# Hybrid decoder trunk on one core: inputs stored feature-major, weights as one stream, values computed token-major ahead of the heads, scores in half-array pairs, heads unrolled in a new order

## The chip, the cores and the metric

One core of a Trainium2 chip. The metric is the device time of one execution in microseconds (us), median of several runs; lower is better. PE is TensorE, ACT ScalarE, DVE VectorE, POOL GpSimd, SP SyncE (it issues nearly all DMAs).

## The reference

Two layers, 512 tokens, 1024 features, float32. Layer 0 mixes by causal differential attention with 8 heads, layer 1 by pooled causal means over 2, 4, 8 and 16 tokens. Each layer goes on with a convolutional gated MLP (2816 wide) and a gated embedding; a final RMS norm ends it. The attention is the part that the change rewrites:

```python
qkv = xn @ w_qkv                                   # xn = rmsnorm(x, g), 512 x 1024
lam = exp(sum(lam_q1*lam_k1)) - exp(sum(lam_q2*lam_k2)) + lambda_init
s = einsum('bhcqd,bhckd->bhcqk', q_blk, k) * ATTN_SCALE   # 8 heads, components c = 0, 1, head_dim 64
a = softmax(where(causal, s, -inf))
w = a[:, :, 0] - lam * a[:, :, 1]
o = einsum('bhqk,bhkv->bhqv', w, v)                # v of a head is 128 wide
o = rmsnorm(o, sub_g) * (1 - lambda_init)
h = x + o.reshape(B, S, 1024) @ w_o
```

## The kernel before, in words

**Products.** Float32 products are made exact enough by splitting each operand into a high part (rounded to the matmul's 32-bit format, `_hi`) and the rest (`_lo`), and adding three matmuls: hi x hi, hi x lo, lo x hi (`exact`, lines 1182 to 1184). One call takes a 128x128 block of weights and 512 moving columns and accumulates in one of 8 PSUM banks.

**Weight units.** Weights come in units of up to 8 blocks (512 KB). SP loads a unit into `w_raw`; ACT writes `w_hi` (`split_hi`), then DVE writes `w_lo` (`split_lo`), and a counter `lo_done` lets PE use it. ACT and DVE do this at fixed places of their own instruction order, one or two units ahead of PE. Attention uses three slots (q, k, v of a head), everything later four.

**Order.** Each engine has its own written-out order, and semaphores tie them. The start (`start_rest` and the lines ahead of `head`): x arrives token-major, PE transposes it (L1219, 32 transposes), ACT and DVE make `x_hi` and `x_lo` scaled by the gain; parameters and p are also transposed on PE (L1319, L1327). The token norm is not applied to x: its inverse goes into the softmax scale and into k and v (multiplied by `inv`, a 128x512 tile that PE spreads from a diagonal, L1301/L1302).

Then 8 heads, each on PE: q projection (24 matmuls), k projection (24), transposes of the last head's v (4, L1270) and of its softmax weights (10, L1278), the spread of the norm of the head before that (L1301), v projection (24), the last head's product weights x v (`head_product`, 12), this head's scores, and within them the sums of squares for the last head's output norm (L1296). Heads 2 to 7 are a hardware loop.

**Scores** (lines 1251 and 1253). `q_hi` holds for each component c its 64 rows and a copy in the other 64; `k_hilo` holds k's high part in the one half and its low part in the other. So one matmul with 128 rows gives q_hi x (k_hi + k_lo), and a second adds q_lo x k_hi: two matmuls for each query tile (width 128, 256, 384, 512) and component, plus masks as bf16 matmuls with an identity (L1256, L1259) behind them.

**After the heads.** The output projection `wo` has 8 units. Its first three accumulate over the finished heads while head 7's softmax, weights, product and norm are still under way; `wo_part(m, heads)` is one such piece. Everything after it (embedding, MLP, pooling, second layer) is some 900 us of matmuls that the change leaves as they are, except for a counter's offsets.

## Time and profile before

| what | value |
| --- | --- |
| median of 3 runs | 1131.6 us (1131.04 to 1131.61) |
| the profiled execution | 1132.1 us, its span 1130.4 us |
| PE busy | 1111.5 us (98%), 5201 matmuls |
| DVE, ACT busy | 753.7 us (67%), 559.8 us (50%) |
| granted PE clock, mean | 0.995 of full speed |
| DMA | 103.57 MB, 92 GB/s on average |

The span is what the profile covers; 1.7 us lie around it. Busy PE time counts pipelined matmuls with a modelled end, so that the distance between two starts says what a matmul really takes. The heads lie between 13.8 and 208.5 us, the output projection behind them.

### The profile page before, as it was taken

How to read it: one execution, taken by the hardware profiler on the slowest of the kernel's cores; microseconds unless marked ns; L12 is line 12 of the kernel's file. 1: busy time of each engine (PE TensorE's matmuls, PEld its weight loads, DVE VectorE, ACT ScalarE, POOL GpSimd, SP SyncE). 2: the span in 40 equal slices, each digit the busy share in tenths (PEclk: the TensorE clock that was granted, in tenths of full speed). 3: DMA queues.
4: the chain of work that ended last, by engine and by line, in shares of the span. 5: the costliest groups of instructions: out<-in, count | busy, mean ns of one | idle time of the engine just before them, and what ended most of it. 6: DMA issues, size and time to landing. Idle time of an engine off the chain costs nothing.

```text
span 1130.4 us, 14839 instructions
## 1 busy us (share of the span) xinstructions
PE 1111.5 (98%) x5201; PEld 924.4 (82%) x5201; DVE 753.7 (67%) x1080; ACT 559.8 (50%) x832; POOL 9.0 (1%) x57
## 2 busy tenths in 40 slices
PE   7999999999999999999999999999999999999996
PEld 6888888888888888888888888888888888888885
DVE  5878788765776347752676787777537774476773
ACT  7777776746554224431444577544314442244564
POOL 0000000002000000000000000000000000000000
PEclk9999999999999999999999999999999999999998
DMA  7232113132333423333323432133323333232411
GB/s 218 70 88 61 56 56 93 57 104 83 93 93 100 120 79 93 93 113 92 93 75 98 126 93 76 57 97 108 112 75 93 98 107 112 75 88 84 126 38 75
DMA packets 192544, 103.57 MB, mean 92 GB/s; under 512 B 3651, under 2 KB 190452, under 8 KB 192500
## 3 DMA queue, kind: packets, MB, share of 16 engines
q1 hardware_dynamic: 192484, 102.99, 30.9%
q8 instruction: 26, 0.43, 0.2%
q14 instruction: 18, 0.15, 0.0%
q10 hardware_dynamic: 16, 0.00, 0.0%
HBM read 100.89 MB, written 2.10 MB: 91 GB/s over the span
## 4 chain that ended last, share of the span: by engine, by line
PE 96%; ACT 1%; DMA 1%; DVE 0%; issue 0%; SPq 0%; ACTq 0%
PE bank L1182 30%; PE bank L1184 30%; PE bank L1183 30%; PE bank L1251 1%; PE bank L1253 1%; PE bank L1296 1%; DMA x_tok<-in_x 1%; PE bank L1278 1%; PE bank L1475 0%; PE bank L1270 0%; PE bank L1472 0%; PE bank L1207 0%; PE bank L1301 0%; PE bank L1302 0%; PE bank L1256 0%
## 5 line engine op out<-in xcount | busy, mean ns | idle before, releaser
L1182 PE MATMUL bank<-x_hi,w_hi 128*128 128x512 f32 x1024 | 400.9, 391 | 1.5 <-DVE h L798 1.5
L1184 PE MATMUL bank<-x_hi,w_lo 128*128 128x512 f32 x1024 | 399.3, 390 | 0.0
L1183 PE MATMUL bank<-x_lo,w_hi 128*128 128x512 f32 x1024 | 399.0, 390 | 0.0
L1182 PEld LDWEIGHTS bank<-x_hi,w_hi 128*128 128x128 f32 x1024 | 192.7, 188 | 41.3 <-issue 1.7
L1184 PEld LDWEIGHTS bank<-x_hi,w_lo 128*128 128x128 f32 x1024 | 192.5, 188 | 40.3
L1183 PEld LDWEIGHTS bank<-x_lo,w_hi 128*128 128x128 f32 x1024 | 192.7, 188 | 39.6
L423 ACT ACTIVATE w_hi<-w_raw 128x1024 fp32r<-128x1024 f32 (+1 forms) x166 | 169.5, 1027 | 102.9 <-PE bank L1184 102.9
L781 DVE TENSOR_TENSOR w_lo<-w_raw,w_hi 128x1024 fp32r<-128x1024 f32 (+1 forms) x166 | 198.0, 1194 | 33.7 <-ACT w_hi L423 33.5
L1182 PE MATMUL bank<-g_hi,w_hi 128*128 128x512 f32 x352 | 136.9, 389 | 0.0
L1183 PE MATMUL bank<-g_lo,w_hi 128*128 128x512 f32 x352 | 136.9, 389 | 0.0
L1184 PE MATMUL bank<-g_hi,w_lo 128*128 128x512 f32 x352 | 136.9, 389 | 0.0
L677 ACT ACTIVATE c<-u,params 128x512 f32<-128x512 f32 x88 | 71.9, 817 | 107.6 <-DVE u L1104 107.6
L1104 DVE TENSOR_TENSOR u<-bank,inv 128x512 f32<-128x512 f32 x88 | 60.7, 689 | 93.3 <-PE bank L1184 93.2
L1002 DVE TENSOR_TENSOR h<-bank,h 128x512 f32<-128x512 f32 x56 | 38.5, 688 | 97.9 <-PE bank L1184 97.9
L684 ACT ACTIVATE g_hi<-g 128x512 f32 (+1 forms) x44 | 27.8, 633 | 118.4 <-DVE g L1120 118.4
L1182 PEld LDWEIGHTS bank<-g_hi,w_hi 128*128 128x128 f32 x352 | 66.1, 188 | 13.7
L1183 PEld LDWEIGHTS bank<-g_lo,w_hi 128*128 128x128 f32 x352 | 66.1, 188 | 13.7
L1184 PEld LDWEIGHTS bank<-g_hi,w_lo 128*128 128x128 f32 x352 | 66.1, 188 | 13.7
L1114 DVE SCALAR_TENSOR_TENSOR c<-u,params,c 128x512 f32<-128x512 f32 x88 | 66.2, 752 | 9.7 <-DVE c L1109 0.9
L1109 DVE SCALAR_TENSOR_TENSOR c<-u,params,c 128x512 f32<-128x512 f32 x88 | 66.0, 750 | 2.3 <-ACT c L677 0.9
L682 ACT ACTIVATE s<-c 128x512 f32<-128x512 f32 x44 | 27.8, 633 | 74.6 <-DVE c L1114 74.6
L1122 DVE TENSOR_TENSOR g_lo<-g,g_hi 128x512 f32 (+1 forms) x44 | 30.5, 693 | 37.7 <-ACT g_hi L684 37.7
(196 smaller groups left out, 1116.1 us busy)
## 6 DMA issues: line engine op xcount, KB each, us to landing
w_raw<-in_w_up SPq DMA_DIRECT2D x88, 512.0 KB, 3.8
w_raw<-in_w_down SPq DMA_DIRECT2D x32, 512.0 KB, 3.5
w_raw<-in_w_qkv SPq DMA_DIRECT2D x24, 512.0 KB, 4.4
w_raw<-in_w_ple_gate SPq DMA_DIRECT2D x16, 512.0 KB, 3.5
w_raw<-in_w_down SPq DMA_DIRECT2D x16, 384.0 KB, 3.1
w_raw<-in_w_attn_out SPq DMA_DIRECT2D x8, 512.0 KB, 3.7
x_tok<-in_x SPq DMA_DIRECT2D x4, 512.0 KB, 5.3
w_raw<-in_w_ple_proj SPq DMA_DIRECT2D x4, 512.0 KB, 4.0
```

Of the source, the lines that this page charges most:

```text
L423: act.activation(w_hi[s][:, 0:w], w_raw[s][:, 0:w], ACT.Copy).then_inc(hi_done, 1)
L677: act.activation(c32[:, c, :], u32[:, c, PAD:PAD + SEQ], ACT.Identity, scale=tap(layer, 2, j + c * FT), bias=conv_bias(layer, j + c * FT)) ...
L682: act.activation(s32[:, :], c32[:, 0, :], ACT.Silu).then_inc(silu_done, 1)
L781: dve.tensor_tensor(w_lo[s][:, 0:w], w_raw[s][:, 0:w], w_hi[s][:, 0:w].bitcast(F32), ALU.subtract).then_inc(lo_done, 1)
L1002: dve.tensor_tensor(h[:, m, :], src, h[:, m, :], ALU.add).then_inc(evac_done, 1)
L1104: dve.tensor_tensor(u32[:, c, PAD:], bank[2 * v + c][:, :], inv[:, :], ALU.mult).then_inc(evac_done, 1)
L1109: dve.scalar_tensor_tensor(out=c32[:, c, :], in0=u32[:, c, PAD - 1:PAD - 1 + SEQ], scalar=tap(layer, 1, j + c * FT), in1=c32[:, c, :], op0 ...
L1114: dve.scalar_tensor_tensor(out=c32[:, c, :], in0=u32[:, c, PAD - 2:PAD - 2 + SEQ], scalar=tap(layer, 0, j + c * FT), in1=c32[:, c, :], op0 ...
L1122: dve.tensor_tensor(g_lo[:, 2 * a + v, :], g32[:, :], g_hi[:, 2 * a + v, :].bitcast(F32), ALU.subtract).then_inc(glo_done, 1)
L1182: pe.matmul(dst, w1, m1, start=start and i == 0, stop=False)
L1183: pe.matmul(dst, w1, m0, start=False, stop=False)
L1184: last = pe.matmul(dst, w0, m1, start=False, stop=stop and i == len(parts) - 1)
```

## The change

**Layout.** The host hands over x and p feature-major, the parameters as one table of columns, and all weights as one array of 166 units of 128 x 1024, in the order of use. PE's transposes of x, p and the parameters are gone; x goes by DMA straight into `h`. The sum of squares of x, before an accumulating ACT pass over `x_tok`, is now made like the other norms: squares on ACT, adds on DVE, then `token_sums` on PE.

**v first.** The first 8 units are v's weights. Tokens are the stationary side, so v comes out token-major for all heads (2 groups of 4 heads, 8 steps k of 12 matmuls each: 192 matmuls, as many as before) and needs no transposes. The inverse norm is a scale per partition (`value_high`, `value_low`). Then each head projects k, then q; a ring of four slots serves all units.

**Scores.** q and k are stored once. Three half-array matmuls (64 rows) for each query tile and component: q_hi x k_hi, q_hi x k_lo, q_lo x k_hi, component 0 on rows 0 to 63 and component 1 on rows 64 to 127, into different banks, issued in turn. The masks go first.

**Softmax.** The weights are kept unnormalized: ratio = lam * sum0 / sum1, w = ratio*a1 - a0, one DVE pass in place of two; a term with sum0 squared goes into the output norm's epsilon (`output_variance`), and the sign into `sub_g_scaled`.

**Order.** The heads are unrolled, the softmax weights are transposed in the middle of the q projection, and the last head's pieces of `wo` are put in another order.

```diff
@@ score banks and matmuls
-                return bank[2 + qt][:, c * w:(c + 1) * w]
+                return bank[2 + c][:, qt * P:qt * P + w]
...
-                        pe.matmul(dst, q_hi[:, c, keys], k_hilo[:, c, 0:w], start=not (shared and c), stop=False,
-                                  skip_group_check=shared)
-                        pe.matmul(dst, q_lo[:, c, keys], k_hilo[:, c, 0:w], start=False, stop=False, skip_group_check=shared)
...
+                    for q, k, stop in ((q_hi, k_hi, False), (q_hi, k_lo, False), (q_lo, k_hi, True)):
+                        for c in range(2):
+                            last = pe.matmul(scores_at(qt, c), q[half[c], keys], k[half[c], 0:w], start=False, stop=stop,
+                                             skip_group_check=True)
@@ ACT between the value groups
+            split_hi(4)
+            rms_of(NORM_MIX0)
+            act.wait_ge(icol_done, 1)
+            for t in range(TT):
+                value_high(t)
+            split_hi(5)
+            inverse(NORM_MIX0)
+            act.wait_ge(p_in, 16)
+            for j in range(DEPTH * PLE_KT):
+                act.activation(pT_hi[:, j, :], p_raw[:, j, :], ACT.Copy).then_inc(pT_hi_done, 1)
+                if j == 0:
+                    split_hi(6)
@@ PE, the values
+            for k in range(1, KT):
+                values(0, k)
+            pe.wait_ge(acc_done, KT)
+            token_sums(bank[7], acc).then_inc(ss_done, 1)
+            for k in range(KT):
+                values(1, k)
+                if k == 3:
+                    pe.wait_ge(diag_done, 1)
+                    pe.wait_ge(vlo_done, 1)
+                    spread(bank[0]).then_inc(spread_done, 1)
@@ PE, a head
+            for hd in range(N_HEADS):
+                n = FIRST_KQ + 2 * hd
...
+                project(bank[1], n, range(KT))
...
+                    project(bank[0], n + 1, range(0, KT // 2))
                     head_transposes(hd - 1)
+                    project(bank[0], n + 1, range(KT // 2, KT))
+                if hd >= 2:
+                    output_spread(hd - 2)
+                if hd >= 1:
+                    pe.wait_ge(k32_done, hd + 1)
+                    head_product(hd - 1, bank[1])
+                scores(hd)
+                if hd >= 1:
+                    output_sums(hd - 1, bank[0])
@@ DVE, a head
+            for hd in range(N_HEADS):
+                split_lo(FIRST_KQ + 2 * hd + 2)
+                k_rows(hd)
+                if hd >= 2:
+                    output_inverse(hd - 2)
+                k_low(hd)
+                if hd >= 1:
+                    transposed_low(hd - 1)
+                split_lo(FIRST_KQ + 2 * hd + 3)
+                q_low(hd)
+                if hd >= 2:
+                    output_norm(hd - 2)
+                    output_low(hd - 2)
+                softmax_first(hd)
+                if hd >= 1:
+                    output_variance(hd - 1, bank[0])
+                softmax_second(hd)
@@ ACT and PE, the last head
+            output_rms(last - 1)
+            transposed_high(last)
+            split_hi(PHASES["wo"][0] + 2)
+            output_high(last - 1)
+            output_square(last, bank[2])
+            output_copy(last, bank[2])
+            split_hi(PHASES["wo"][0] + 3)
...
+            head_transposes(last)
+            output_spread(last - 1)
+            wo_part(2, range(0, last - 1), start=True)
+            head_product(last, bank[2])
+            wo_part(3, range(0, 2), start=True)
+            output_sums(last, bank[4])
+            wo_part(3, range(2, last - 1))
```

How the order stands on the engines at three places. **First**, ACT where the norm of x is turned into a tile, before: the tile `inv` comes behind q's high part, and no unit of weights that PE wants next stands behind it.

```order
L429 ACTIVATE w_hi<-w_raw 128x1024 [waits raw_in2]
L480 ACTIVATE q_hi<-bank 64x512 [waits unit_done]
L480 ACTIVATE q_hi<-bank 64x512
L483 ACTIVATE q_hi<-q_hi 64x512 [waits qhi_done] x2
L437 ACTIVATE inv<-bank 128x512 [waits spread_done]
L488 ACTIVATE k_hilo<-k 64x512 [waits k32_done]
```

Now, ACT at the same tile (`w_hi2` there is unit 6, which PE uses at step k = 4 of the second group of values):

```order
L351 ACTIVATE w_hi1<-w_raw1 128x1024 [waits unit_done,raw_in1]
L359 ACTIVATE inv<-bank0 128x512 [waits spread_done]
L406 ACTIVATE pT_hi<-p_raw 128x512 [waits p_in]
L351 ACTIVATE w_hi2<-w_raw2 128x1024 [waits unit_done,raw_in2]
L406 ACTIVATE pT_hi<-p_raw 128x512 x3
```

The split of unit 6 stands behind the tile, and the tile waits for the spread, which PE issues after step k = 3, right ahead of step k = 4.

**Second**, PE at the scores of heads 2 to 7, before (k and q are the moving and the stationary side):

```order
L1182 MATMUL bank6<-wT_hi,v_hi 128x128 [waits wtlo_done]
...
L1251 MATMUL bank2<-k_hilo,q_hi 128x128 [waits wtlo_done]
L1253 MATMUL bank2<-k_hilo,q_lo 128x128
...
L1259 MATMUL bank2<-mask16,ident16 128x256
...
L1251 MATMUL bank6<-k_hilo,q_hi 128x512 [waits onorm_done,o32_done]
```

and now:

```order
L1080 MATMUL bank1<-wT_hi,v_hi 128x128 [waits wtlo_done]
...
L1187 MATMUL bank2<-mask16,ident16 128x2x128 [waits onorm_done,klo_done,qlo_done]
L1187 MATMUL bank3<-mask16,ident16 128x2x128
L1191 MATMUL bank4<-mask16,ident16 128x128
...
L1197 MATMUL bank2<-k_hi,q_hi 128x128
L1197 MATMUL bank3<-k_hi,q_hi 128x128
```

The first score matmul now waits for `onorm_done` (the normed output of two heads before, for its bank 6) and `qlo_done`; before, `onorm_done` was waited for four query tiles later.

**Third**, PE in the last head, before:

```order
L1182 MATMUL bank6<-wT_hi,v_hi 128x512 [waits wtlo_done,vlo_done]
...
L1182 MATMUL bank2<-oT_hi,w_hi1 128x512 [waits lo_done,wtlo_done]
...
L1301 MATMUL bank7<-diag,ones_r 128x512 [waits odiag_done,onorm_done]
L1302 MATMUL bank7<-diag,ones_r 128x512
L1182 MATMUL bank3<-oT_hi,w_hi2 128x512 [waits lo_done]
```

PE now, and ACT beside it:

```order
L1117 MATMUL bank6<-diag,ones_r 128x512 [waits odiag_done]
L1118 MATMUL bank6<-diag,ones_r 128x512
L1080 MATMUL bank7<-oT_hi,w_hi2 128x512 [waits lo_done]
...
L1080 MATMUL bank2<-wT_hi,v_hi 128x512 [waits wtlo_done]
...
L1080 MATMUL bank3<-oT_hi,w_hi3 128x512 [waits lo_done]
```

```order
L428 ACTIVATE wT_hi<-bank2 128x512 [waits w_T]
L428 ACTIVATE wT_hi<-bank3 128x384 [waits w_T]
L428 ACTIVATE wT_hi<-bank4 128x384 [waits w_T]
L351 ACTIVATE w_hi2<-w_raw2 128x1024 [waits unit_done,raw_in2]
L434 ACTIVATE oT_hi<-acc 128x512 [waits onorm_done]
L438 ACTIVATE sq<-bank2 128x512 [waits pv_done]
L445 ACTIVATE acc<-bank2,small 128x512 [waits olo_done]
L351 ACTIVATE w_hi3<-w_raw3 128x1024 [waits unit_done,raw_in3]
```

The third piece of `wo` (bank 7, `w_hi2`) moved ahead of the head's product and its weights are split behind the transposed softmax weights; the fourth (bank 3, `w_hi3`) moved to right behind the product, and its weights are split behind the square that waits for that product.

## Rows read from the trace of the kernel before

**Rows 1.** The page, part 1: busy us (share of the span), instructions.

```profile
PE 1111.5 (98%) x5201; PEld 924.4 (82%) x5201; DVE 753.7 (67%) x1080; ACT 559.8 (50%) x832; POOL 9.0 (1%) x57
```

**Rows 2.** Waits of PE: line and releaser: us, times, longest.

```profile
PE bank L1182 <- DVE h L798: 1.5, 1, 1.5
PE bank L1182 <- DVE wT_lo L939: 0.5, 1, 0.5
```

**Rows 3.** Timeline (start us, us, operation), start; window with clock, its seventh entry.

```profile
4.26 1.06 ACT L446 ACTIVATE square_scratch<-x_tok 128x1024 f32<-128x1024 f32 x1 [1.54 <-DMA x_tok<-in_x]
13.77 0.77 PE L1182 MATMUL bank<-x_hi,w_hi 128*128 128x512 f32 x1 [1.50 <-DVE h L798]
16.47 0.51 PE L1182 MATMUL bank<-x_hi,w_hi 128*128 128x512 f32 x1
...
14.00:16.00 2.00, 2.00 (x5) 1.56 (x6) 1.97 (x4) 2.00 (x5) 0.00 (x0) 0.50 0.15 37
```

**Rows 4.** Timeline of PE through one head.

```profile
123.77 0.39 PE L1182 MATMUL bank<-x_hi,w_hi 128*128 128x512 f32 x1
129.24 0.39 PE L1182 MATMUL bank<-wT_hi,v_hi 128*128 128x512 f32 x1
131.10 0.27 PE L1251 MATMUL bank<-k_hilo,q_hi 128*128 128x128 f32 x1
132.26 0.95 PE L1296 MATMUL bank<-ones,sq 128*128 128x1 f32 x8
133.08 0.42 PE L1251 MATMUL bank<-k_hilo,q_hi 128*128 128x384 f32 x1
135.22 0.48 PE L1182 MATMUL bank<-x_hi,w_hi 128*128 128x512 f32 x1
```

**Rows 5.** Timeline, PE: transposes and spread ahead of Rows 4.

```profile
121.77 0.60 PE L1270 MATMUL bank<-ident,vT 128*128 128x128 f32 x4
122.21 1.25 PE L1278 MATMUL bank<-ident,probs 128*128 128x128 f32 x10
123.22 0.48 PE L1301 MATMUL bank<-diag,ones_r 128*128 128x512 f32 x1
```

**Rows 6.** Timeline, end of the start: spread, parameters, lambda.

```profile
26.39 0.39 PE L1302 MATMUL bank<-diag,ones_r 128*128 128x512 f32 x1
26.82 0.60 ACT L437 ACTIVATE inv<-bank 128x512 f32<-128x512 f32 x1 [1.74 <-PE bank L1302]
28.83 0.29 PEld L1332 LDWEIGHTS bank<-lam_rows,ones 64*128 64x128 f32 x2 [0.17 <-issue]
29.14 0.50 PE L1182 MATMUL bank<-x_hi,w_hi 128*128 128x512 f32 x1
```

**Rows 7.** Timeline of the same head, ACT.

```profile
134.07 1.28 ACT L519 ACT_TABLE_LOAD   x1
135.36 0.46 ACT L519 ACTIVATE probs<-bank,small 128x128 f32<-128x128 f32 x1
137.33 0.68 ACT L519 ACTIVATE probs<-bank,small 128x384 f32<-128x384 f32 x1
140.14 1.08 ACT L429 ACTIVATE w_hi<-w_raw 128x1024 fp32r<-128x1024 f32 x1
```

**Rows 8.** Timeline of the same head, DVE.

```profile
132.53 1.02 DVE L889 TENSOR_REDUCE small<-bank 128x2 f32<-128x256 f32 x2 [0.80 <-PE bank L1259]
135.44 1.29 DVE L893 TENSOR_REDUCE small<-bank 128x1 f32<-128x512 f32 x2 [0.16 <-PE bank L1256]
143.99 1.23 DVE L787 TENSOR_TENSOR w_lo<-w_raw,w_hi 128x1024 fp32r<-128x1024 f32 x1
145.14 0.17 DVE L944 RECIPROCAL small<-small 128x4 f32<-128x4 f32 x1
147.00 0.69 DVE L875 TENSOR_TENSOR k<-bank,inv 128x512 f32<-128x512 f32 x1
150.44 1.61 DVE L939 TENSOR_TENSOR wT_lo<-bank,wT_hi 128x512 fp32r<-128x512 f32 x3
```

More of the change, by code:

```diff
@@ L279, in hybrid_trunk @@
         sums = small[:, 32:40]
-        rsums = small[:, 40:48]
+        sums_of = [sums.rearrange("p (t c) -> p t c", c=2)[:, :, c] for c in range(2)]
+        rsum = small[:, 40:44]
+        ratio = small[:, 44:48]
         rms_col = small[:, 48:52]
@@ L477, in q_high @@
-            def q_high(hd):
-                act.wait_ge(unit_done, 3 * hd + 1)
-                for c in range(2):
-                    act.activation(q_hi[own[c], c, :], bank[0][own[c], :], ACT.Copy).then_inc(qhi_done, 1)
-                for c in range(2):
-                    act.wait_ge(qhi_done, 2 * hd + c + 1)
-                    act.activation(q_hi[other[c], c, :], q_hi[own[c], c, :].bitcast(F32), ACT.Copy).then_inc(qtwin_done, 1)
+                act.activation(inv[:, :], bank[7 if norm else 0][:, :], ACT.Copy, scale=float(D_MODEL)).then_inc(inv_done, 1)
@@ new lines, in token_sums, with spread @@
+            def token_sums(dst, squares):
+                for t in range(TT):
+                    last = pe.matmul(dst[:, t:t + 1], squares[:, t * P:(t + 1) * P], ones[:, 0:1], start=True, stop=True)
+                return last
+            def spread(dst):
+                pe.matmul(dst[:, :], ones_r[:, :], diag[:, 0, :], start=True, stop=False)
+                return pe.matmul(dst[:, :], ones_r[:, :], diag[:, 1, :], start=False, stop=True)
+            TOK = [slice(t * P, (t + 1) * P) for t in range(TT)]
@@ L1409, in norm_sums @@
             def norm_sums(norm):
[L1410 removed]
+                pe.wait_ge(acc_done, KT * (norm + 1))
                 token_sums(bank[7], acc).then_inc(ss_done, 1)
```

820 lines of the change are left out of this document (367 added, 453 removed).

## Prediction

> **What bounds the kernel now.** The page says PE: 98% busy [rows 1]. Such a share can hide pipelining, so I read next who keeps PE waiting: from its first projection on hardly anyone, and the two waits ahead of the output projection's middle that I use are 1.5 us for the first x tiles and 0.5 us for the transposed weights of the last head [rows 2]. Then the timeline of the start: the first useful matmul starts at 13.77, though the first 512 KB of x had landed at 4.26; the rest was transposing. It runs at half the clock (granted 0.50, the 1.2 GHz level) until about 16.5 [rows 3]. Last the timeline of one head, which gives prices. Distances between starts count, not durations: 24 projection matmuls take 129.24 - 123.77 = 5.47, 0.228 each; the product 1.86; the scores 1.16 and 2.14, together 3.30; the sums between them 0.82 [rows 4]. Ahead of them lie 0.44 for v's transposes, 1.01 for the ten of the weights, 0.55 for the spread [rows 5]. A head is thus 72 x 0.228 + 8.0 = 24.4 us, without a gap. So what PE is spared counts in full, and so does every wait put in its way. With 1100 us of PE work the kernel's end moves only with PE's.
>
> **What PE is spared.**
> 1. Start. The first value matmuls want 256 KB of x and 256 KB of weights, as much as had landed by 4.26 [rows 3]; then ACT copies two tiles of 512 columns (0.6 each by the `inv` row, [rows 6]), so PE starts at about 5.3: -8.5 us. Bounds 4.9 and 7.0. The slow clock of the first 2.7 us is paid in both. From there PE needs 2.7 us for each 512 KB, which arrived in less than 2 us each before, and ACT and DVE have 4 us of work per 5.4 us: nothing starves.
> 2. Parameters and p: from the end of the spread (26.39 + 0.23) to 29.14 are 2.5 us [rows 6]; 0.3 for lambda stays and sums of squares of 0.82 come in: -1.4.
> 3. v's transposes: 8 x 0.44 = -3.5. The values themselves are 192 matmuls of 512 columns in both: 0.
> 4. Scores. 16 matmuls and 6 masks took 3.30. 5120 columns at 0.228 per 512 are 2.3; short ones are held up by their weights, so I put 2.5 on the matmuls and 0.8 on the masks. If the two halves of a pair run at once, 12 steps replace 16: 1.9. Masks in a row cost perhaps 0.6, and going to half the rows and back something: the only 64-row load shows 0.17 of idle ahead of it [rows 6], so 0.25 for both ways. Sum 2.75, a gain of 0.55 a head, -4.4 in all. Bounds: 2.4 a head, and 4.65 with no overlap at all.
>
> The Trainium skill ("TensorE: Matmul & The Clock Gate", Part 3) has row-packed matmuls run concurrently, a few ns apart, and "TensorEngine Tiling (Array Packing)", Key Properties, says that a change of the tiling mode drains the array. By the first a pair is one step, by the second the switch costs; no row before shows a pair.
>
> **What PE has to wait for now.** These I worked out as schedules from the rows, engine by engine.
> 5. Between step k = 3 and 4 of the second value group. PE's spread, then ACT makes `inv` (it starts 0.43 after the spread's second matmul, [rows 6]), copies one tile of p (together 1.05), and only then splits unit 6 (1.05, [rows 7]); DVE's part is 1.2 [rows 8]. PE could go on 0.23 after that matmul and goes on 3.9 after it: +3.65. Nothing else of PE's order stands in between.
> 6. Head 0: its scores follow the q projection at once, so q's copy and rest (0.6 + 0.7 + 0.4 to get from PE to ACT) are bare: +1.65. Before, the v projection covered them.
> 7. Heads 1 to 7, ahead of the scores. Count from the start of a head's scores. The first two query tiles are done at 1.5, DVE sees them 0.25 later and needs 1.2 for four reductions (1.02 for two double ones, [rows 8]), 0.2 for the negation; then two pairs, 1.0 and 1.3 [rows 8], 0.2: 5.65. The second four exponentials take 140.14 - 137.33 = 2.8 [rows 7]: 8.45. ACT then loads a table (1.28), takes a root (0.22) and splits a unit (1.05) [rows 7]: 11.0. DVE: rest of the unit 1.15 (143.99 to 145.14), k 0.6, the inverse and diagonal 1.86 (145.14 to 147.00), k's rest 0.6, the weights' rest 1.6, another unit 1.15, q's rest 0.6, the output norm 0.7 [rows 8]: 8.25, ends at 19.25, and the next scores wait for it. That is the least period of a head. PE's own work in a period is 10.9 + 1.0 + 0.55 + 1.86 + 2.75 + 0.82 = 17.9. So PE waits 1.4 in each: 7 x 1.4 = +9.8. With the v projection of 5.47 in the loop there was slack; taken out, the chain over ACT and DVE is the bound and half of the gain of item 4 is only room for it. Bounds of the wait: 0 (if the chain is 1.4 shorter) and 2.2.
> 8. Last head. PE's third piece of `wo` needs unit 2, split by ACT behind the weights' high parts. From the first transpose: ACT has those at 2.0, the split at 3.05, DVE at 4.3; PE is at 1.6: +2.8. The fourth piece needs unit 3, whose split stands behind the square that waits for the head's product: 0.2, a square 0.5, a copy 0.6, the split 1.05, DVE 1.2, latencies: +3.7. The norm's chain ends 0.3 after PE gets to it. The old wait of 0.5 goes [rows 2]. Together +6.3. PE has no other work in its order at these places.
>
> Sum: -8.5 - 1.4 - 3.5 - 4.4 + 3.65 + 1.65 + 9.8 + 6.3 = +3.6 us. Against the profiled execution's 1132.1 (span 1130.4) that is 1135.7; the median of the runs, 1131.6, is 0.5 lower, so I say 1135.2. The DMA side costs nothing: SP's queue of loads stays ahead, because ACT's splits wait for PE, not for weights. DVE's second pass over the softmax (gone), the doubled q and k copies on ACT (gone) and the bigger weight packets are already in the schedules or off the path; what is left of the program is the same work in the same order.
>
> **The rivals.**
> - B, pairs overlap but their weight loads don't: a 128-column load limits short steps to about 0.11, so a pair takes 0.225 whatever its width: scores 3.55. The least period grows by the first part only, 0.65 a head, 0.8 in head 0: +5.3, 1140.5. For: each half matmul has its own load. Against: nothing in the rows.
> - C, no overlap: 24 steps, scores 4.65. PE's work grows by 1.9 a head, the waits shrink from 1.4 to 0.2: +6.8, 1142.0.
> - D, faster: the chain of item 7 is shorter than PE's work, because DVE's backlog drains in time: it decides at 17.9 us a period, against 19.25 in my schedule. Then the waits of 9.8 are gone: 3.6 - 9.8 = -6.2, 1125.4, and 1124 with an earlier start and cheaper masks. For: every length is from a kernel in which these engines had slack, and six of eight steps are judged by like ones. Against: 1.4 of 19.25 is much, with no single step that large in doubt.
> - E, the clock. PE idles for 3.65, 2.8 and 3.7 us at items 5 and 8. Before, the clock was at half after the wait of 1.5 that followed sparse transposes [rows 2, 3]. At half speed for 2.7 us PE loses some 1.3: three times +4.0, 1139.2. The Trainium skill ("TensorE: Matmul & The Clock Gate") has the clock fall back when PE sits idle for long enough; by that rule this case is likely, by the rows it is open.
>
> **How the numbers follow.** Forecast 0.33, B 0.18, C 0.12, D 0.23, E 0.14. A change of 0.2%, 2.3 us, is about what a measurement of this kernel can tell from none: faster means below 1129.3, slower above 1133.9. The forecast's own spread is 3 us to either side (start 0.5, waits 2, masks and switch 1.5): a tenth of it is faster, four tenths the same. D is faster in nine of ten, else the same. B, C and E are slower. Faster 0.24, same 0.15, slower 0.61. The range reaches into D and to C and leaves out a tenth at each side: 1125 to 1142; the forecast's own is 1132 to 1138.
>
> **What would show it.** In the trace of the changed kernel: first matmul at 5.3; no more rows of transposed x, p and v; PE waits for `w_lo` once of 3.65 in the values, and of 2.8 and 3.7 in the last head; a head's period of about 19.3 with a wait of 1.4 behind `acc` or `q_lo` ahead of the mask matmuls; scores of 2.75 with a pair's two starts close together. Starts of a pair 0.11 or more apart at every width say B, at the distance of their own columns C. A period near 18 says D. A granted clock of 0.5 behind the long waits says E. I am wrong about the whole if the waits of items 5 and 8 are not there, for they are 10 of the 21.4 us that stand against the gains of 17.8.

## The result, and the profile after

The changed kernel takes 1143.4 us (median of 4 runs, 1142.3 to 1144.9), the kernel before 1131.6 (1131.0 to 1132.0): ratio 1.0105, 95% interval 1.0088 to 1.0123. It is slower, by 11.8 us; the forecast was 3.6 us, and the range ended at 1142. The profiled execution took 1144.9 us with a span of 1143.1, against 1132.1 and 1130.4. The four times stand in two pairs, 1142.3 and 1142.4 and then 1144.4 and 1144.9, and the kernel before has such steps of some 2 us too, so a difference of under 2 us between single kernels is not clear.

The page of the changed kernel, part 1 (busy us, share of the span, instructions), the clock row of part 2, and the start of part 4, the chain that ended last:

```profile
PE 1107.2 (97%) x5188; PEld 919.5 (80%) x5188; DVE 731.9 (64%) x1071; ACT 536.6 (47%) x795; POOL 9.0 (1%) x56
PEclk9999999989999999999999999999999999999997
PE 84%; DVE 7%; ACT 7%; issue 1%; DMA 0%; ACTq 0%
```

PE is busy for only 4 us less by this count [rows 1], though it was spared 17.8 us of its time. The two don't measure the same, since PE was busy for half of the old start only, but part of the saving is eaten by matmuls that take longer: one digit of the clock row is an 8. The chain runs over DVE and ACT for 14% of the span; before, PE alone was 96% of it.

Waits of PE in the changed kernel (line and releaser: us, times, longest):

```profile
PE bank L1080 <- DVE w_lo L706: 10.2, 4, 3.5
PE bank L1128 <- ACT x_hi L366: 6.3, 1, 6.3
PE bank L1187 <- DVE acc L869: 4.1, 6, 0.7
PE bank L1187 <- DVE q_lo L812: 1.9, 2, 1.4
PE bank L1080 <- DVE h L909: 1.1, 1, 1.1
```

Beside [rows 2] this is a different kernel: four waits for a weight's low part, one wait ahead of each head's scores (1.4 us in head 0, 0.5 and 0.7 in the others), and one of 1.1 us for a result to leave its bank.

The places of the long ones, in PE's timeline (start us, us, operation, idle before and releaser), with what follows them:

```profile
6.29 2.05 PE L1128 MATMUL bank<-w_hi,x_hi 128*128 128x512 f32 x4 [6.29 <-ACT x_hi L366]
...
11.33 0.40 PE L1080 MATMUL bank<-w_hi,x_hi 128*128 128x512 f32 x1
...
37.71 0.50 PE L1080 MATMUL bank<-w_hi,x_hi 128*128 128x512 f32 x1 [0.78 <-DVE w_lo L706]
...
43.57 0.39 PE L1118 MATMUL bank<-diag,ones_r 128*128 128x512 f32 x1
47.36 0.50 PE L1080 MATMUL bank<-w_hi,x_hi 128*128 128x512 f32 x1 [3.41 <-DVE w_lo L706]
...
49.06 0.63 PE L1080 MATMUL bank<-w_hi,x_hi 128*128 128x512 f32 x1
49.49 0.63 PE L1081 MATMUL bank<-w_lo,x_hi 128*128 128x512 f32 x1
...
219.28 0.79 PE L1080 MATMUL bank<-oT_hi,w_hi 128*128 128x512 f32 x1 [2.53 <-DVE w_lo L706]
219.87 0.63 PE L1081 MATMUL bank<-oT_lo,w_hi 128*128 128x512 f32 x1
220.30 0.63 PE L1082 MATMUL bank<-oT_hi,w_lo 128*128 128x512 f32 x1
...
230.55 0.79 PE L1080 MATMUL bank<-oT_hi,w_hi 128*128 128x512 f32 x1 [3.47 <-DVE w_lo L706]
231.14 0.63 PE L1081 MATMUL bank<-oT_lo,w_hi 128*128 128x512 f32 x1
```

Read the distances: behind the waits of 3.41, 2.53 and 3.47 us matmuls of 128x512 come to stand 0.43 us apart, where they stand 0.23 apart elsewhere [rows 4]. The windows of the same trace (stretch: length, busy us of PE, its weight loads, DVE, ACT and POOL, then granted clock, DMA share, GB/s) say why, and for how long; the last is the end of PE's work, ahead of the final output:

```profile
48.00:52.00 4.00, 4.00 (x14) 3.18 (x12) 1.12 (x2) 0.91 (x1) 0.00 (x0) 0.57 0.37 131
219.00:223.00 4.00, 3.72 (x9) 2.98 (x10) 1.52 (x3) 0.63 (x1) 0.00 (x0) 0.57 0.34 131
229.00:240.00 11.00, 9.45 (x27) 7.76 (x28) 3.12 (x6) 0.44 (x2) 0.00 (x0) 0.53 0.13 48
1131.00:1135.00 4.00, 2.83 (x12) 2.42 (x12) 0.18 (x1) 2.37 (x5) 0.00 (x0) 0.50 0.00 0
```

A granted clock of 0.57 over 4 us takes away 4 x 0.43 = 1.7 us, and 0.53 over 11 us takes 11 x 0.47 = 5.2, but part of that lies in the waits, where it costs nothing. What the matmuls lost is read from starts, against the trace of experiment 10, in which the same work runs at full speed. From the spread ahead of v's wait to head 0's masks it is 72.66 - 43.57 = 29.09 us against 27.59; from the third piece to the end of the head's product 7.5 against 6.0; from the fourth piece to the next spread 240.64 - 230.55 = 10.09 against 5.86. So the 1.2 GHz level costs 1.5, 1.5 and 4.2 us behind the three waits.

One head, PE's timeline (to be held against [rows 4]):

```profile
126.75 0.27 PE L1082 MATMUL bank<-wT_hi,v_lo 128*128 128x128 f32 x1
127.72 0.38 PE L1187 MATMUL bank<-mask,ident 128*128 128x256 bf16 x2 [0.69 <-DVE acc L869]
...
129.57 0.39 PE L1197 MATMUL bank<-k_hi,q_hi 64*128 64x512 f32 x2
129.80 0.40 PE L1197 MATMUL bank<-k_lo,q_hi 64*128 64x512 f32 x2
130.36 1.05 PE L1112 MATMUL bank<-ones,sq 128*128 128x1 f32 x8
...
146.59 0.38 PE L1187 MATMUL bank<-mask,ident 128*128 128x256 bf16 x2 [0.71 <-DVE acc L869]
```

A head takes 146.59 - 127.72 = 18.87 us. Its scores, masks to sums, take 130.36 - 127.72 = 2.64 instead of 3.30; x2 in a row is a pair of matmuls, one on each half. The last matmul of the product would have let the next one start at 126.87, so the gap ahead of the masks is 0.85 us.

Where the 12.7 us between the two spans lie, from four landmarks that both traces have:

| stretch | before | after | difference | forecast |
|---|---|---|---|---|
| from the start of the span to the first matmul of the output projection | 208.6 | 206.8 | -1.8 | -2.7 |
| from there to the sums of the norm behind it | 55.7 | 68.6 | +12.9 | +6.3 |
| from there to the last sums over `acc` | 853.5 | 853.5 | 0 | 0 |
| from there to the end | 12.6 | 14.2 | +1.6 | 0 |

So the first stage came out nearly as summed, though not by the terms that were written down. The miss is in the output projection: 6.6 us, of which 5.8 are the 1.2 GHz level (1.5 and 4.2 from starts; from one spread to the next 24.5 against 18.8 in experiment 10). A remainder is at the end.

### The profile page after: what moved, and what is told of

The parts are those of the page before. It is cut to its first block, busy times and chain, and to the rows that moved or that the text cites. A ratio compares the mean times of both kernels' runs of the same rounds, so it can differ in the third digit from the quotient of the medians.

```text
span 1143.1 us, 14467 instructions
## 1 busy us (share of the span) xinstructions
PE 1107.2 (97%) x5188; PEld 919.5 (80%) x5188; DVE 731.9 (64%) x1071; ACT 536.6 (47%) x795; POOL 9.0 (1%) x56
## 4 chain that ended last, share of the span: by engine, by line
PE 84%; DVE 7%; ACT 7%; issue 1%; DMA 0%; ACTq 0%
PE bank L1080 27%; PE bank L1081 27%; PE bank L1082 27%; ACT probs L457 2%; DVE w_lo L706 2%; ACT w_hi L351 1%; DVE wT_lo L852 1%; DVE diag L724 1%; ACT L449 1%; PE bank L1112 1%; DVE small L827 1%; ACT L457 1%; DVE q_lo L812 0%; DVE acc L869 0%; DVE oT_lo L874 0%
## 5 line engine op out<-in xcount | busy, mean ns | idle before, releaser
L1080 PE MATMUL bank<-x_hi,w_hi 128*128 128x512 f32 x960 | 375.7, 391 | 0.0
L1082 PE MATMUL bank<-x_hi,w_lo 128*128 128x512 f32 x960 | 373.9, 389 | 0.0
L1081 PE MATMUL bank<-x_lo,w_hi 128*128 128x512 f32 x960 | 373.6, 389 | 0.0
L706 DVE TENSOR_TENSOR w_lo<-w_raw,w_hi 128x1024 fp32r<-128x1024 f32 (+1 forms) x189 | 225.9, 1197 | 45.3 <-ACT w_hi L351 45.1
L351 ACT ACTIVATE w_hi<-w_raw 128x1024 fp32r<-128x1024 f32 (+1 forms) x189 | 193.5, 1030 | 102.6 <-PE bank L1082 102.6
L1082 PEld LDWEIGHTS bank<-x_hi,w_lo 128*128 128x128 f32 x960 | 180.2, 188 | 37.8
L1080 PEld LDWEIGHTS bank<-x_hi,w_hi 128*128 128x128 f32 x960 | 180.3, 188 | 37.0 <-issue 0.4
L1081 PEld LDWEIGHTS bank<-x_lo,w_hi 128*128 128x128 f32 x960 | 180.3, 188 | 36.7
```

What stands on the lines that cost most here:

```text
L351: act.activation(w_hi[s][:, 0:w], w_raw[s][:, 0:w], ACT.Copy).then_inc(hi_done, 1)
L706: dve.tensor_tensor(w_lo[s][:, 0:w], w_raw[s][:, 0:w], w_hi[s][:, 0:w].bitcast(F32), ALU.subtract).then_inc(lo_done, 1)
L1080: pe.matmul(dst, w1, m1, start=start and i == 0, stop=False)
L1081: pe.matmul(dst, w1, m0, start=False, stop=False)
L1082: last = pe.matmul(dst, w0, m1, start=False, stop=stop and i == len(parts) - 1)
```

## The experiments

All start from the changed kernel. The ratios are to the kernel before, run again beside each experiment (medians of 1131.9 to 1133.6 us). The changed kernel wasn't run again, so what an edit gave is a difference to its first four runs, 1142.3 to 1144.9; where it is small, the traces decide. Two theories: **clock** (the waits are about as forecast, and behind a long one PE runs at half speed for some us, which no term had) and **waits only** (the slow matmuls have another cause, and the missing us are waits mis-sized).

**1. Early splits in v.** `split_hi(5)` and `split_hi(6)` on ACT, and their `split_lo` on DVE:

```diff
-            for t in range(TT):
-                value_high(t)
-            split_hi(5)
+            value_high(0)
+            split_hi(5)
+            for t in range(1, TT):
+                value_high(t)
+                if t == 2:
+                    split_hi(6)
             inverse(NORM_MIX0)
```

> The changed kernel with the splits of v's units 5 and 6 set ahead of value_high/value_low of the second and fourth bank, on ACT and on DVE. In the changed kernel PE waits 0.8 us at 37.71 and 3.4 us at 47.36 (gaps of 0.94 and 3.56 between matmuls), and from 48.4 to 51.9 its matmuls stand 0.43 us apart where 0.23 is usual, which loses about 1.5 us. Theory (a wait costs its length and the slow matmuls behind it): both waits go and with them the slow stretch, first k projection at 54.3 instead of 60.2, 1137.4 us. Rival (only the waits count; the slow stretch comes from something else and stays): 1138.9 us. Second rival (the next split or value_low is late in their place and the wait only moves): above 1141 us.

Measured: 1136.2 us (1135.5 to 1138.4), 1.0036 of before (1.0024 to 1.0049). The waits at k = 2 and 4 are gone and no slow stretch is left in v; one of 0.76 us for unit 7 took their place. Head 0's masks start at 67.83 instead of 72.66. These 4.8 us are what the edit gave. The rest of the 7.2 came elsewhere: in this profiled execution the output projection was 4.6 us shorter too, since the clock stayed up behind the first wait of the output projection and was down for a shorter time behind the second. Windows of both stretches:

```profile
214.00:218.00 4.00, 3.53 (x15) 2.93 (x16) 1.71 (x3) 0.63 (x1) 0.00 (x0) 1.00 0.38 131
223.00:228.00 5.00, 3.83 (x15) 3.25 (x16) 1.19 (x2) 0.00 (x0) 0.00 (x0) 0.66 0.31 105
```

The waits there are the same 2.54 and 3.47 us as in the changed kernel. So the same wait may or may not be followed by a slow stretch, and the loss is no constant that could be added per wait. That the total hit the forecast is partly luck.

**2. Early splits in the output projection.** On ACT (on DVE `split_lo` of the third piece ahead of `transposed_low(last)`, of the fourth behind it):

```diff
+            split_hi(PHASES["wo"][0] + 2)
+            split_hi(PHASES["wo"][0] + 3)
             transposed_high(last)
-            split_hi(PHASES["wo"][0] + 2)
             output_high(last - 1)
             output_square(last, bank[2])
             output_copy(last, bank[2])
-            split_hi(PHASES["wo"][0] + 3)
```

> The changed kernel with the splits of the output projection's third and fourth piece set ahead of the last head's transposed_high on ACT, and on DVE ahead of and behind transposed_low. In the changed kernel PE waits 2.53 us at 219.28 and 3.47 us at 230.55, and its matmuls stand 0.43 us apart for about 3 us behind the first and about 9 us behind the second. Theory: both waits (6.0) and the slow stretches (some 6) go; the transposes' split is pushed back by at most 1.2 us of DVE, so a wait of up to 1 us may stand before the product; 1131.5 to 1132.5 us. Rival (only the waits count): 1137.4 us, with slow matmuls still in the output projection. In either case the wait before the last output_low remains.

Measured: 1131.5 us (1131.2 to 1133.1), 0.9991 (0.9982 to 1.0001). 11.9 us gained by moving two copies and two subtractions: the two waits of 6.0 us together and the 5.8 us behind them. No wait came in their place.

**3. The waits kept, but filled.** This one tells the theories apart: matmuls that compute nothing used stand where PE would stand still.

```diff
+            for _ in range(11):
+                pe.matmul(bank[5][:, :], ones_r[:, :], diag[:, 1, :], start=True, stop=True)
             wo_part(2, range(0, last - 1), start=True)
             head_product(last, bank[2])
+            for _ in range(15):
+                pe.matmul(bank[5][:, :], ones_r[:, :], diag[:, 1, :], start=True, stop=True)
             wo_part(3, range(0, 2), start=True)
```

> The changed kernel, its order kept, with 11 matmuls of 128x512 into an unused bank in front of the output projection's third piece and 15 in front of its fourth: they fill the two waits (2.5 and 3.5 us at 0.227 us each), compute nothing that is used, and leave every wait in place. Theory (the clock falls because PE stands still): the two waits shrink to under 0.2 us, matmuls behind them stand 0.23 apart, and the time falls by the slow stretches alone, some 6 us, to 1137.4 us. Rival (the slow stretches have another cause, the matmuls of these pieces or their place in the program): no change from 1143.4 us within 1 us, 0.43-us steps where they were.

Measured: 1137.6 us (1137.4 to 1137.9), 1.0041 (1.0026 to 1.0055). PE's timeline there, and the window over both pieces (v's, whose wait isn't filled, stands ahead of it):

```profile
215.59 2.69 PE L1283 MATMUL bank<-diag,ones_r 128*128 128x512 f32 x11
218.30 0.50 PE L1080 MATMUL bank<-oT_hi,w_hi 128*128 128x512 f32 x1
218.64 0.40 PE L1081 MATMUL bank<-oT_lo,w_hi 128*128 128x512 f32 x1
218.87 0.39 PE L1082 MATMUL bank<-oT_hi,w_lo 128*128 128x512 f32 x1
```
```profile
46.00:51.00 5.00, 4.67 (x15) 3.73 (x15) 2.08 (x4) 1.86 (x3) 0.00 (x0) 0.66 0.30 105
215.00:233.00 18.00, 17.99 (x87) 14.60 (x86) 7.26 (x12) 4.95 (x9) 0.00 (x0) 1.00 0.17 58
```

The real work waits just as long as it did, yet the granted clock stays at 1.00 and 5.8 us are gone, in the trace as in the median. It is PE's standing still that brings the clock down at these places, and here that costs as much as the waits themselves.

**4. The waits filled by half.** 5 and 7 matmuls in the place of 11 and 15:

```diff
-            for _ in range(11):
+            for _ in range(5):
...
-            for _ in range(15):
+            for _ in range(7):
```

> As the kernel whose two waits in the output projection were filled with 11 and 15 matmuls, but with 5 and 7, so that PE still stands still for about 1.4 and 1.9 us there. The full fill gave 1137.6 us and no slow stretch behind. The waits of 0.7 us at each head have no slow stretch behind them. Theory (a standstill has to reach some length, between 0.9 and 2.5 us, before the clock falls): 1137.6 us if 1.9 us is short enough; rival (how long it stood is what matters less than that it stood at all in that stage): a slow stretch behind at least one of them, 1139 to 1143 us.

Measured: 1137.7 us (1137.6 to 1137.8), 1.0040 (1.0025 to 1.0056), waits of 1.38 and 1.80 us left. The window over them:

```profile
214.00:235.00 21.00, 17.82 (x90) 14.52 (x89) 7.76 (x14) 5.27 (x9) 0.00 (x0) 1.00 0.16 50
```

A standstill of 1.8 us after busy work cost only itself, as those of 0.7 in the heads do. No wait under 2.5 us between the start and the last norm had a slow stretch behind it in these profiles; of those of 2.5 and more, most did. Outside of these bounds that doesn't hold: behind a wait of 1.5 us ahead of the last sums the clock was at 0.50 in the changed kernel and up in the kernel before.

**5. The wait ahead of a head's scores.** DVE's split of a head's second unit goes from ahead of `q_low` to between the two halves of `softmax_second`.

```diff
-                split_lo(FIRST_KQ + 2 * hd + 3)
                 q_low(hd)
...
-                softmax_second(hd)
+                softmax_second(hd, FIRST_KQ + 2 * hd + 3)
...
                 for pair in range(2):
+                    if pair:
+                        split_lo(ahead)
```

> The changed kernel with DVE's split of a head's second unit moved from ahead of q_low to the middle of softmax_second, where DVE waits 1.6 us for the exponentials. Theory (the wait ahead of a head's scores is the end of DVE's chain, w_lo split, q_low, output_norm): q_low and output_norm come 1.2 us earlier, the wait of 0.86 us before each head's scores goes, a head takes 18.0 us instead of 18.88, and the time falls by 6 x 0.86 + 1.42 + 0.47 less a rest, 5 to 6.5 us, to 1137.5 us. Rival (the bound is output_norm's spread or ACT's exponentials, not DVE's queue): under 1.5 us gained, period 18.6 or more.

Measured: 1137.6 us (1135.3 to 1139.5), 1.0033 (1.0019 to 1.0047). PE's timeline of the same head:

```profile
126.96 0.28 PE L1083 MATMUL bank<-wT_hi,v_lo 128*128 128x128 f32 x1
127.08 0.39 PE L1188 MATMUL bank<-mask,ident 128*128 128x256 bf16 x2
129.73 1.05 PE L1113 MATMUL bank<-ones,sq 128*128 128x1 f32 x8
...
145.10 0.39 PE L1188 MATMUL bank<-mask,ident 128*128 128x256 bf16 x2
```

A head now takes 145.10 - 127.08 = 18.02 us and no scores wait but head 0's, 1.4 us as before. The 1.2-us subtraction fills time in which DVE waits for exponentials. The loop over ACT and DVE was the bound by 0.85 us, through the order of DVE's queue and not through the amount of its work.

**6. The scores' terms of one half in a row.** Three matmuls on one half of the rows, then three on the other:

```diff
-                    for q, k, stop in ((q_hi, k_hi, False), (q_hi, k_lo, False), (q_lo, k_hi, True)):
-                        for c in range(2):
+                    for c in range(2):
+                        for q, k, stop in ((q_hi, k_hi, False), (q_hi, k_lo, False), (q_lo, k_hi, True)):
```

> The changed kernel with the score matmuls of one half array in a row (for each query tile all three terms of the first half, then all three of the second) instead of in turn. Same matmuls, same count. In the changed kernel twelve pairs of 64-row matmuls step by 0.11, 0.12, 0.17 and 0.23 us a pair for widths 128 to 512 (1.9 us in all), and the stretch from masks to sums is 2.64 us. Theory (two neighbours on different half arrays run side by side, which makes a pair cost one): without neighbours the 24 matmuls take up to twice 1.9, so 1.5 to 1.9 us more a head, 12 to 15 us in all, about 1157 us. Rival (a 64-row matmul is cheap by itself, neighbours or not): within 2 us of 1143.4.

Measured: 1142.2 us (2 runs, 1139.9 and 1144.5), 1.0082 (1.0052 to 1.0112): no change that is clear, and in the trace masks to sums take 2.64 as before. The theory as I put it, only neighbours overlap, has fallen. Two readings are left, that halves run side by side without being neighbours, or that a 64-row matmul is cheap.

**7. All scores on one half.** Both sets are taken from the first half's rows, so the second half's scores are not computed.

```diff
-  q[half[c], keys], k[half[c], 0:w]
+  q[half[0], keys], k[half[0], 0:w]
```

> The changed kernel with the score matmuls of the second half taken from the first half's rows as well: both score sets are then the first half's, the number and the widths of the matmuls stay. All 24 stand on the same half of the array. Setting the terms of one half in a row changed nothing (1142.2 us), which leaves two readings. Theory (matmuls on different halves run side by side, neighbours or not): on one half they can't, 1.5 to 1.9 us more a head, masks to sums 4.2 to 4.5 us instead of 2.64, about 1157 us. Rival (a 64-row matmul costs half of a full one wherever it stands): 2.64 us and 1142 to 1144 us as before.

Measured: 1158.0 us (2 runs, 1155.2 and 1160.8), 1.0214 (1.0182 to 1.0246). PE's timeline of one head's scores:

```profile
133.03 0.39 PE L1187 MATMUL bank<-mask,ident 128*128 128x256 bf16 x2
...
136.11 0.62 PE L1197 MATMUL bank<-k_hi,q_hi 64*128 64x512 f32 x2
136.57 0.62 PE L1197 MATMUL bank<-k_lo,q_hi 64*128 64x512 f32 x2
...
137.58 1.05 PE L1112 MATMUL bank<-ones,sq 128*128 128x1 f32 x8
```

Two matmuls of 512 columns on one half step by 0.46 us, 0.23 each, as a full-array one does; on different halves a pair steps by 0.23. Masks to sums take 4.55. So the halves do run at the same time in the changed kernel, which spares PE 1.9 us a head; the two needn't be neighbours, three of one half may come before three of the other. That the median hit the forecast is again partly luck, and the two runs are 5.6 us apart. I had counted 1.9 a head as lost time, but 0.85 of it only fills the wait ahead of the scores, which is gone (two scores stand 19.94 us apart, 1.07 more than in the changed kernel). In the trace the heads take 12.8 us more, and 3.3 of these are the clock, which falls twice with no wait of PE ahead, once right behind the scores and sums of the head at 111:

```profile
112.00:116.00 4.00, 4.00 (x26) 3.46 (x24) 2.88 (x8) 3.29 (x8) 0.00 (x0) 1.00 0.20 77
117.00:121.00 4.00, 4.00 (x12) 3.17 (x12) 2.04 (x9) 3.49 (x11) 0.00 (x0) 0.57 0.00 0
```

**8. Work ahead of the first matmul.** 36 matmuls of 128x128, while the first x and weights arrive:

```diff
             pe.wait_ge(const_done, 3)
+            pe.wait_ge(ones_done, 1)
+            for _ in range(36):
+                pe.matmul(bank[7][:, 0:P], ones_r[:, :], ones_r[:, :], start=True, stop=True)
             first_values()
```

> The changed kernel with 36 matmuls of 128x128 (ones by ones, into a bank not yet used) between the arrival of the ones and the first matmul at 6.29; they compute nothing that is used. In the changed kernel the first twelve 128x512 matmuls stand 0.42 us apart and take 5.04 us where 2.7 would do. Theory (the clock rises once PE has worked a while, whatever it works on): the twelve take 2.7 to 3.4 us, and v's first steps then meet the splits of x, with waits of some 0.5 us: 1 to 2.3 us gained, 1141.7 us. Rival (that work bounds the start, since x and w arrive when they do: DVE's x_low and w_lo set the pace until 11 us): under 0.5 us gained, new waits in the place of the slow steps.

Measured: 1148.1 us (1143.0 to 1148.6), 1.0119 (1.0092 to 1.0147): worse by 4.7 (3.7 between the two profiled executions), both theories missed. The 36 took 7.7 us, 0.21 each, so the first product stood behind them until 9.86 instead of 6.29, and the twelve slow ones behind took 5.1 us all the same:

```profile
2.15 7.91 PE L1156 MATMUL bank<-ones_r 128*128 128x128 f32 x36 [2.15 <-DVE ones_r L710]
9.86 2.01 PE L1128 MATMUL bank<-w_hi,x_hi 128*128 128x512 f32 x4
...
14.96 0.40 PE L1080 MATMUL bank<-w_hi,x_hi 128*128 128x512 f32 x1
```

**9. The same with 9 of 128x512.**

```diff
+            for _ in range(9):
+                pe.matmul(bank[7][:, :], ones_r[:, :],
+                          ones_r[:, :].rearrange("p (o c) -> p o c", o=1).broadcast_to((P, TT, P)), start=True, stop=True)
```

> As the kernel with 36 matmuls of 128x128 ahead of the first one, but with 9 of 128x512 (ones read four times over). The 36 took 7.9 us, put the first product matmul off from 6.29 to 9.86 and the twelve behind them were as slow as ever (5.1 us). Nine at 0.42 us end at 5.9 us. Theory (wide matmuls, which the twelve are, bring the clock up, narrow ones do not): the step falls from 0.42 to 0.23 us by about 7 us, 1 to 2.3 us gained, 1141.5 us; PE then meets x_low and w_lo of the first tiles. Rival (the clock rises at a time counted from the first product, or at 11 us whatever PE does): slow until 11 us, 1143.4 us.

Measured: 1142.1 us (1141.4 to 1142.8), 1.0077 (1.0060 to 1.0094), 1.3 better, which the medians alone don't show; in the trace the first norm's sums come at 28.79 instead of 30.41:

```profile
2.15 4.18 PE L1156 MATMUL bank<-ones_r 128*128 128x512 f32 x9 [2.15 <-DVE ones_r L710]
6.38 1.70 PE L1128 MATMUL bank<-w_hi,x_hi 128*128 128x512 f32 x4
7.93 1.07 PE L1131 MATMUL bank<-w_lo,x_hi 128*128 128x512 f32 x4
```

The step falls to 0.23 at 7.9, and the twelve take 3.4 us instead of 5.0. In the three runs the slow speed lasted 5.0 (changed kernel), 5.1 (behind the 36) and 5.8 us (the nine included) from the first matmul of 128x512 on. What ends it isn't settled; the records of this stretch grant the full clock (1.00 from 6 to 12 in the changed kernel) while the steps are those of half speed.

**10. Everything filled, every wait kept.** Experiments 3 and 9 together, 15 matmuls in v's wait (in `values`, below), and ahead of the waits for `acc` and for the last square:

```diff
+                if g == 1 and k == 4:
+                    pe.wait_ge(vlo_done, 2)
+                    for _ in range(15):
+                        pe.matmul(bank[1][:, :], ones_r[:, :], x_hi[:, 0, :], start=True, stop=True)
                 pe.wait_ge(lo_done, n + 1)
...
+            for _ in range(2):
+                pe.matmul(bank[4][:, :], ones_r[:, :], diag[:, 1, :], start=True, stop=True)
             pe.wait_ge(acc_done, KT * (NORM_FINAL + 1) - 1)
...
+            for _ in range(6):
+                pe.matmul(bank[4][:, :], ones_r[:, :], diag[:, 1, :], start=True, stop=True)
             pe.wait_ge(sq_done, KT * (NORM_FINAL + 1))
```

> The changed kernel, its order and all its waits kept, with matmuls that compute nothing used standing in the long ones: 9 of 128x512 ahead of the first product, 15 in v's second group ahead of the fifth step, 11 and 15 in the output projection, 2 and 6 ahead of the last sums. From the changed kernel's 1143.4 us go what the trace has as lost to half speed: 1.6 at the start (as measured with the nine alone), 1.7 behind the 3.4-us wait in v, 6.8 in the output projection (less some 1 where other runs had less), 1.3 at the end. Theory (the forecast's waits were right in sum and the clock is what it lacked): 1132 to 1134 us, the sum of the waits alone being within 2 us of zero against before. Rival (waits mis-sized as well): 1136 us or more.

Measured: 1134.1 us (1133.9 to 1135.0), 1.0017 (1.0007 to 1.0026). Windows over v's wait and over the output projection:

```profile
46.00:51.00 5.00, 5.00 (x24) 4.09 (x24) 2.68 (x6) 3.33 (x5) 0.00 (x0) 1.00 0.34 105
214.00:240.00 26.00, 24.74 (x112) 19.46 (x112) 9.09 (x14) 6.93 (x11) 0.00 (x0) 1.00 0.17 59
```

With the order of the changed kernel and all its waits, but with PE at full speed from about 8 us on, the change costs 2.5 us (0.8 to 2.9 by the interval, against the kernel before run beside it). The other 9.3 us came back with nothing but work put where PE stood still. The forecast's sum without the clock was 3.6. The two aren't quite the same thing: experiment 10 also shortens the slow start, by 1.3 (experiment 9) to 2.1 us (its own trace), and the sum counted the start as slow, as it is in the kernel before. With that added back the change would cost about 4 us, an estimate from these runs.

**11. The edits together.** Experiments 1, 2 and 5.

> The changed kernel with three edits together: the early splits of v's units 5 and 6, the early splits of the output projection's third and fourth piece, and the head's second split in softmax_second. Each alone gave 1136.2, 1131.5 and 1137.6 us. Theory (the waits stand in different stages and add up; slow stretches in the output projection were partly in two of the three gains): v 5.0, output projection 12 and heads 5.7 from 1143.4 us gives 1120.7 us, 1 % faster than before the change. Rival (a shared bound, such as ACT's exponentials, turns up once the heads' waits go): 1124 us or more.

Measured: 1120.3 us (1120.1 to 1122.3), 0.9894 (0.9877 to 0.9911). They add up, less the slow stretches that were in more than one of the single gains, and the result beats the kernel before by 11.3 us with no matmul added.

**12. Small edits on top.** Unit 7 of v split early, the first result of the output projection evacuated ahead of the fifth piece's split on DVE, the 36 matmuls at the start, 2 and 6 ahead of the last sums; then the same without the 36. The first two, on ACT (DVE's `split_lo` alike) and in DVE's `residual_phase`:

```diff
-                if t == 2:
-                    split_hi(6)
+                if t >= 2:
+                    split_hi(t + 4)
...
-                    if m + look < KT + LOOK:
+                    if m + look < KT + LOOK and not first:
                         split_lo(n + look)
...
                     residual_add(m, bank[WO_BANKS[m % SLOTS] if name == "wo" else m % SLOTS][:, :])
+                    if first:
+                        split_lo(n + look)
```

> The three edits together, and four small ones: v's unit 7 split ahead of the spread's inverse (0.76 us of wait in the kernel with early v splits), the output projection's first result taken out of its bank ahead of the split of the fifth piece (0.7 of the 1.1 us wait at 247.56), 36 matmuls to fill PE's time before its first matmul, and 2 and 6 to fill its waits before the last sums. Theory: 0.8, 0.7, 1 to 2.3 and 1 to 2 us less than the three together: 1120.7 - 4.5 = 1116.2 us. Rival for the last (the clock falls there at whatever the chip finds, not because PE waits): 1117.5 us.

> The three edits with the early unit 7, the earlier result of the output projection's first piece and the filled waits before the last sums, without the 36 matmuls at the start. With them the kernel took 1121.3 us, and its sums of the first norm stood at 33.08 instead of 30.33. Theory (the four small edits cost and give what they did in the trace, each by itself: 0.8 and 0.7 given, 2.75 taken): 1118.6 us. Rival (the filled waits at the end cost what they give): 1119.3 us or more.

Measured: 1121.3 us (1121.2 to 1121.4), 0.9898 (0.9881 to 0.9914), 5 above its forecast and 1 above experiment 11, and without the 36 1118.6 us (1118.3 to 1119.2), 0.9866 (0.9850 to 0.9883). In the trace the 36 put the first norm's sums off by 2.75 us (33.08 against 30.33), and leaving them out gave back 2.8.

**13. The best version.** As the last, with the nine of 128x512 at the start.

> The best version so far (1118.6 us) with the nine matmuls of 128x512 ahead of the first product as well. They gave 1.3 us in the changed kernel (1142.1 against 1143.4), and the first norm's sums came at 28.8 instead of 30.4. Theory (the start's gain is passed on whole, since PE waits nowhere between the start and the heads): 1117.1 us. Rival (v's splits, now early, or the spread's chain are late at the faster start, and a wait takes the gain back): 1118.6 us.

Measured: 1116.7 us (1116.5 to 1117.4), 0.9862 (0.9842 to 0.9882). PE's waits in it:

```profile
PE bank L1160 <- DVE ones_r L710: 2.2, 1, 2.2
PE bank L1195 <- DVE q_lo L812: 1.4, 1, 1.4
...
PE bank L1084 <- DVE w_lo L706: 0.4, 1, 0.4
```

It is 14.9 us faster than the kernel before. Some of that is work put into waits that the kernel before has as well, at the start and the end; the fair figure for the change is experiment 11, which only moves splits: 11.3 us faster, where the changed kernel was 11.8 slower. What the change spares PE was real, and the order in which ACT and DVE split the weights lost it.

## Why the prediction was wrong in size

The sign was right, and for the reason given: the work spared was outweighed by waits in new places. The size was wrong by 8.2 us. The step that failed is the sum itself, which put the clock behind the waits of items 5 and 8 at nothing. That half speed stood among the rivals, as E, with 4.0 us and a chance of 0.14. In the profiled execution it costs 1.5 us behind v's wait and 5.8 in the output projection, 7.3 at the places that E names, and 1.3 to 1.6 more at the end, where it had not fallen in the profile of the kernel before. E was the right mechanism at about half its size. It took its price from the start of the kernel before (2.7 us at half speed, 1.3 lost) and multiplied by three; behind the third wait 4.2 were lost. Experiment 3 shows the cause and the amount in the output projection, experiment 10 the amount of all. The Trainium skill ("TensorE: Matmul & The Clock Gate", Part 1), named there, has the clock fall when PE idles for long enough; these traces agree with it, for most waits of 2.5 to 3.5 us. That rule doesn't explain the two falls in experiment 7, where PE hadn't idled.

Term by term, by the prediction's items:

- **Item 1, start, -8.5.** The first product came at 6.29, inside the bounds but 1.0 later than said. A third of that is ACT's copy of x waiting for the gains, whose transfer is behind x on ACT's own queue. And the slow speed, "paid in both" as 2.7 us, lasted 5.0. Together some 2 us too hopeful.
- **Items 2 and 3, parameters and v's transposes**: the rows are gone, no run tests them alone.
- **Item 4, scores, 2.75 a head**: 2.64. The rule that the two halves run at once was taken rightly, and C (no overlap, 4.65 a head) is what experiment 7 measures: 4.55. B fell too: pairs of 128 columns step by 0.11 to 0.16, not 0.225. What changing to half the rows and back costs, 0.25 in the sum, was not measured alone.
- **Item 5, v's wait, +3.65**: 47.36 - 43.57 - 0.23 = 3.56, the releaser as said. "Nothing else of PE's order stands in between" was wrong: unit 5's split stands behind four `value_high` and held PE 0.9 us at 37.71.
- **Item 6, head 0, +1.65**: 1.42.
- **Item 7, heads 1 to 7, +9.8**: 0.85 in six of them and 0.5 in head 1, some 5.6. Of the 0.55 missing in each, 0.4 is the chain being shorter, a period of 18.87 against the 19.25 of the schedule, and the rest PE's own work being 18.0 and not 17.9. Experiment 5 shows that the bound named was the right one. D, in which these waits vanish, needed a chain that is another 0.85 shorter.
- **Item 8, last head, +6.3**: the gaps are 2.7 and 3.6 against 2.8 and 3.7. One wait more, 1.1 us at 247.56, wasn't in the sum: the fifth piece needs a bank that DVE empties only behind a split.

The terms of opposite sign nearly cancel: the heads 4.2 too dear, start, v and the output projection 1.0, 0.9 and 1.1 too cheap without the clock. That is why the sum without the clock, 1135.2, is close to what experiment 10 gives, 1134.1, or 1135.4 with the 1.3 us of the start added back. That is luck in part, and no proof of each term.

The chance was misplaced as well. E was treated as a case beside the forecast, as if the clock's fall and the forecast's waits excluded each other, though it follows from those waits. Added to the sum at its own price it would have given 1139.2, still 4.2 short, and the same 4.0 on top of case C gives an upper end of 1146.

## What to carry to other kernels

When a change puts a wait of some us into the path of a TensorE that was never idle, price it at its length and again for the matmuls behind it, and put it into the sum and not beside it: here three waits of 9.9 us in all cost 7.3 us more behind them in one profile, and less in some others. Then look at what the wait is for: here each long one was a weight's split that stood in ACT's and DVE's queues behind work that itself waited for PE, and moving it ahead of that work cost nothing. If a wait can't be moved, a few matmuls that compute nothing keep the clock up, provided that they end before the data comes.

## What the runs showed of the hardware

- Waits of 2.5 to 3.5 us were mostly followed by a stretch at the 1.2 GHz level that lost from 1.2 us (experiment 1, behind the wait of 3.47) to 4.2 us (the same wait in the changed kernel). The wait of 2.54 us was followed by one of 1.5 us in the changed kernel and by none in experiments 1, 5 and 9. Waits of 0.7 to 1.8 us were followed by none between the start and the last norm (the heads of all profiles, experiment 4).
- A wait isn't needed for it: with all scores on one half of the rows (experiment 7) the granted clock was 0.51 from 117 to 120 though PE had not stood still, and it was down again behind 178, each time for some 3 us.
- The eight 128x1 sums ahead of the last norm took 1.87 us in the changed kernel's profile and 1.05 in that of the kernel before, at a granted clock of 0.50 and 1.00, behind the same wait of 1.53 us. What decides between the two is not shown.
- 36 matmuls of 128x128 in 7.7 us ahead of the first product left it as slow as without them; nine of 128x512 in 4.2 us saved 1.7 us behind them.
- Matmuls on the two halves of the array's rows overlap fully at 512 columns (0.23 us a pair against 0.46 on one half), with their weight loads, and in blocks of three as well as in turn.
